# A decoder layer with a mixture of experts: code padding, the final squares, one PSUM bank and three bias loads

## The chip, the cores and the metric

The kernel runs on one core of a Trainium2 chip. TensorE (PE in the profile, PEld for its weight loads) multiplies matrices, VectorE (DVE), ScalarE (ACT) and GpSimd (POOL) do the elementwise work, and SyncE (SP) issues most of the DMAs. Each engine runs its own instruction stream in order, and the streams meet at semaphores. The metric is the device time of one execution in microseconds. Three executions of the kernel before took 2072.66, 2072.96 and 2073.78 us.

## The reference

One layer on 1024 tokens of 1024 features, float32 throughout, and a final RMSNorm:

```
h = rmsnorm(x, norm1_g);  q, k, v, u = split(h @ w_in)            # w_in: 1024 x 2048
attn = differential attention, 4 heads, causal:  softmax(q0 k0) v - lam * softmax(q1 k1) v, then rmsnorm per head
pool = trailing means of u over 2, 4, 8, 16 tokens, minus u, times w_pool, plus b_pool, times pool_scale
x = x + concat(attn, pool) @ w_out
h = rmsnorm(x, norm2_g)
top 4 of 32 experts per token, gates = softmax of the 4 router logits
expert e:  gate = min(h w_gate + b_gate, 7);  up = clip(h w_up + b_up, -7, 7)
           y = (gate * sigmoid(1.702 gate) * (up + 1)) w_down + b_down, times the token's gate
x = x + sum of the expert outputs
return rmsnorm(x, final_g)
```

The final norm needs, for each token, the sum of the squares of its row, the inverse root of the mean (`rstd`), and the product with `rstd` and with `final_g`.

## The kernel before

The tokens are eight blocks of 128 (`TB` = 8). The work has four stages on the time axis of the profile.

**Projection and attention (0 to about 370 us).** `jobs` is a list of TensorE products, each into one PSUM bank: transposes of x, then q, k, v and u. `bank_of(n)` gives the bank of job n: `n % 8` for the early ones, and from `first_late` on (the first block of v is job `first_late`, number 34) alternately two banks, here 1 and 3. Before it writes a bank, PE waits until the last user of that bank has been emptied (`user_before`, `emptied`, in `product`, L1442). Job 33, the last product of k, sits in bank 1 (33 % 8) and is emptied by DVE at L934. Job 27 sits in bank 3.

**Output projection and routing (about 370 to 508 us).** For each block b, PE computes the output projection, DVE adds the residual (`x1_ready`), ACT and DVE make the second norm, PE the router's logits, DVE picks the experts, POOL prepares the gates. SP stores each block's x and h rows to DRAM (L399, L401) and, in its turn for the last block, first waits for `out_mm` and loads the three bias matrices of 32 x 1024 (L397) into rows of `hT`. PE transposes two of them at L1677 once all three have landed (`turn_bias`), then ranks the last block's tokens (L1630). When the routing is done, POOL gathers the first expert's rows (L558).

**Experts (508 to 2054 us).** PE's program holds one body of code for each of 11 widths (128, 132, ... 192 token slots); `choose` (L1749) is a chain of compare-and-branch instructions that jumps to the body of the next expert's width, and each body ends with such a chain. `call` places a prefetch hint (L1760) some time ahead of the branch. A body has six groups of products (L1694, or L1721 at width 128). SP streams the weights. DVE evicts with bias and clip (`gate_in`, `up_in`, `down_in`), ACT does the sigmoid, POOL gathers and scatters rows.

**The end (2031 us on).** When the last but one expert's rows have been added in DRAM, SP reads the eight blocks of x back into `x2` (L439; `x_in[b]` counts the landing of block b). ACT squares and sums each block as it lands (L857, `squares_of_rows`). DVE meanwhile evicts the last expert: `down(0)` and `down(1)` are L1254. After all eight sums, DVE computes `rstd` in 12 small steps (L87 to L100, `rsqrt_mean_dve`). Blocks 0 to 3 (`SCALED` = 4) were multiplied by `final_g` on POOL (L640) and are scaled by ACT (L863); blocks 4 to 7 are done by DVE in one instruction each (`normed_row`, L1363). SP sends the blocks out in a fixed order: 4, 1, 5, 2, 6, 3, 7 (L446 for blocks 4 to 7, L443 for blocks 1 to 3); block 0 goes by an indirect DMA of POOL (L643). The rows of the last expert take a way of their own (`last_rows`): PE transposes the expert's output (L1873) after `down(1)`, DVE adds it to the gathered rows (L1350), ACT squares (L873), DVE makes the inverse root and the product (L1359), and POOL writes those rows over the blocks in `out` (L632), which it may do only after all eight blocks have landed there.

The order on every engine is the order in which the code is written; no scheduler moves it. The two lines that choose the bank and the join before the inverse root are

```
return n % 8 if n < first_late else (1, 3)[(n - first_late) % 2]
dve.wait_ge(squares_f, TB)
```

## Time and profile before

| | before |
|---|---|
| median of 3 runs | 2072.96 us (2072.66 to 2073.78) |
| the profiled execution | 2074.92 us, of which the span of the trace is 2073.2 us |
| PE busy | 2011.8 us, 97% of the span |
| DVE, ACT, POOL busy | 655.5, 283.8, 232.9 us |
| TensorE clock granted | 0.99 of full speed over the span |
| DMA | 500.89 MB, mean 242 GB/s |

PE is busy in all but 61 us of the span, and the experts' stretch is three quarters of it. The profiled execution is 1.96 us longer than the median of the runs; a forecast of a difference is worked out on the profiled execution and then carried to the median.

### The profile page before, as it was taken

To read this page: it belongs to the slowest core of one execution; us is meant where nothing else is said; L and a number is where in the kernel's file an instruction comes from. 1 tells how busy PE (TensorE), PEld (TensorE's weight loads), DVE (VectorE), ACT (ScalarE), POOL (GpSimd) and SP (SyncE) were. 2 spreads that over 40 slices of the span, in tenths; PEclk is the share of its full clock that TensorE was granted. 3 is DMA by queue.
4 is the path that set the end of the run, shared out by engine and by line. 5 is a ranking of instruction groups with operands and counts; after the bars stand their busy time and mean duration, and the time that the engine had idled before them with its cause. 6 is when DMAs were issued, how large, how long until landed. Compare 5 with 4: busy or idle time off the path is not lost.

```text
span 2073.2 us, 32125 instructions
## 1 busy us (share of the span) xinstructions
PE 2011.8 (97%) x13457; PEld 1643.8 (79%) x13458; DVE 655.5 (32%) x1363; ACT 283.8 (14%) x457; POOL 232.9 (11%) x381
## 2 busy tenths in 40 slices
PE   8999988996999999999999999999999999999996
PEld 4444455554998898889788999988888888989996
DVE  3115676443223222222222332222222222222223
ACT  2001245111011001101001010111010100100103
POOL 0001333212000001000001010010000000000103
PEclk9999999997999999999999999999999999999998
DMA  4210022214878879998999988899899998887855
GB/s 173 81 41 1 1 92 84 100 61 152 305 248 305 307 272 322 321 329 296 321 322 318 309 294 272 286 319 335 312 304 322 319 319 310 279 299 260 287 189 199
DMA packets 231449, 500.89 MB, mean 242 GB/s; under 512 B 7766, under 2 KB 8303, under 8 KB 231298
## 3 DMA queue, kind: packets, MB, share of 16 engines
q1 hardware_dynamic: 218880, 454.46, 61.0%
q0 software_dynamic: 12368, 44.26, 8.6%
q8 instruction: 113, 1.85, 0.4%
q14 instruction: 38, 0.31, 0.0%
q10 hardware_dynamic: 50, 0.01, 0.0%
HBM read 463.63 MB, written 35.13 MB: 241 GB/s over the span
## 4 chain that ended last, share of the span: by engine, by line
PE 72%; DMA 1%; DVE 1%; issue 1%; SPq 0%; ACT 0%; POOL 0%; POOLq 0%; DVEq 0%; ACTq 0%
PE ps L1694 57%; PE ps L1721 12%; PE ps L1708 2%; PE ps L1714 1%; PE ps L1701 1%; DMA qk<-x_rows 1%; DMA out<-qk 0%; DVE x L1254 0%; DMA hT<-h_rows,hT 0%; DMA x_rows<-x,hT 0%; DVE qk L1363 0%; SPq L439 0%; DVE xn L1221 0%; ACT hT L821 0%; ACT x L857 0%
## 5 line engine op out<-in xcount | busy, mean ns | idle before, releaser
L1694 PE MATMUL ps<-hT,qk 128*128 128x128 f32 (+8 forms) x4096 | 501.7, 284 | 6.8 <-issue 6.8
L1694 PEld LDWEIGHTS ps<-hT,qk 128*128 128x128 f32 x4096 | 493.5, 192 | 16.6 <-issue 16.0
L1721 PE MATMUL ps<-w_ring,hT 128*128 128x512 f32 x576 | 251.8, 593 | 0.0
L1694 PE MATMUL ps<-hT,u_all 128*128 128x128 f32 (+8 forms) x2048 | 247.7, 282 | 0.0
L1694 PE MATMUL ps<-hT,v 128*128 128x128 f32 (+8 forms) x2048 | 247.7, 282 | 0.0
L1694 PEld LDWEIGHTS ps<-hT,v 128*128 128x128 f32 x2048 | 244.6, 191 | 0.0
L1694 PEld LDWEIGHTS ps<-hT,u_all 128*128 128x128 f32 x2048 | 244.6, 191 | 0.0
L1694 PE MATMUL ps<-hT,w_ring 128*128 128x132 f32 (+7 forms) x1792 | 233.8, 291 | 5.0 <-DVE x L1254 3.6
L1694 PEld LDWEIGHTS ps<-hT,w_ring 128*128 128x128 f32 x1792 | 229.3, 190 | 7.4 <-issue 7.0
L1721 PEld LDWEIGHTS ps<-w_ring,hT 128*128 128x128 f32 x576 | 107.5, 190 | 126.7 <-issue 126.3
L558 POOL DMA_INDIRECT hT<-h_rows,hT x46 | 45.3, 986 | 1148.9 <-issue 672.1
L825 ACT ACTIVATE hT<-hT 128x768 f32<-128x768 f32 x64 | 53.9, 842 | 855.5 <-DVE hT L1235 855.5
L1467 PE MATMUL ps<-hT,w_ring 128*128 128x512 f32 x384 | 168.9, 595 | 1.3 <-DMA w_ring<-in_w_in 1.3
L1467 PEld LDWEIGHTS ps<-hT,w_ring 128*128 128x128 f32 x384 | 71.5, 190 | 86.7 <-issue 83.7
L1241 DVE TENSOR_TENSOR hT<-ps,early 128x512 f32<-128x512 f32 (+1 forms) x64 | 51.7, 808 | 241.3 <-PE ps L1694 234.0
L1232 DVE TENSOR_TENSOR hT<-ps,early 128x512 f32<-128x512 f32 (+1 forms) x64 | 51.7, 808 | 212.9 <-PE ps L1694 191.1
L563 POOL DMA_INDIRECT x_rows<-x,hT x44 | 70.1, 1593 | 266.9 <-ACT x L836 220.1
L821 ACT COPY hT<-ps 128x1024 f32<-128x1024 f32 x64 | 51.2, 800 | 338.8 <-PE ps L1708 298.5
L1262 DVE TENSOR_TENSOR x<-ps,x 128x512 f32<-128x512 f32 x36 | 24.9, 692 | 220.4 <-PE ps L1721 220.4
L1254 DVE TENSOR_TENSOR x<-ps,early 128x768 f32<-128x768 f32 x28 | 26.8, 958 | 193.5 <-PE ps L1694 193.5
L1239 DVE TENSOR_TENSOR hT<-hT 128x512 f32<-128x512 f32 (+1 forms) x64 | 52.4, 818 | 65.8 <-ACT hT L825 65.8
L1203 DVE COPY hT<-ps 128x12 f32<-128x12 f32 x31 | 5.3, 171 | 180.5 <-PE ps L1701 180.5
(250 smaller groups left out, 1470.6 us busy)
## 6 DMA issues: line engine op xcount, KB each, us to landing
w_ring<-in_w_down SPq DMA_DIRECT2D x64, 2048.0 KB, 7.9
qk<-in_w_gate SPq DMA_DIRECT2D x32, 2048.0 KB
qk<-in_w_up SPq DMA_DIRECT2D x32, 2048.0 KB
v<-in_w_gate SPq DMA_DIRECT2D x32, 2048.0 KB, 10.5
u_all<-in_w_up SPq DMA_DIRECT2D x32, 2048.0 KB, 8.7
x<-in_b_down SPq DMA_DIRECT2D x32, 512.0 KB, 11.6
w_ring<-in_w_in SPq DMA_DIRECT2D x3, 2048.0 KB, 9.0
x<-in_x SPq DMA_DIRECT2D x8, 512.0 KB, 12.4
```

The source lines that it names most:

```text
L558: return pool.indirect_dma_start(out=xg[0:n, h, :], out_offset=None, in_=rows.h2[:, :], in_offset=bass.IndirectOffsetOnAxis(ap=tab_e[0:n, ...
L563: return pool.indirect_dma_start(out=rows.x1[:, :], out_offset=bass.IndirectOffsetOnAxis(ap=tab_e[0:n, h:h + 1].bitcast(U32), axis=0), in_ ...
L821: act.copy(xT[:, :, h * P:h * P + n], turned_in[h]).then_inc(xT_ready, 1)
L825: act.activation(sg[:, :, :], gt[:, :, :], ACT.Sigmoid, scale=ALPHA).then_inc(sg_ready, 1)
L1232: dve.tensor_tensor(gt[:, :, 0:n], pair[2 * c % PAIRS][:, :, 0:n], bcast(r.bias[:, 0, 4 * c:4 * c + 4, e], n), ALU.add).then_inc(pair_free, 1)
L1239: dve.tensor_tensor(sg[:, :, 0:n], gt[:, :, 0:n], sg[:, :, 0:n], ALU.mult).then_inc(gate_s, 1)
L1241: dve.tensor_tensor(ut[:, :, 0:n], pair[(2 * c + 1) % PAIRS][:, :, 0:n], bcast(r.bias[:, 1, 4 * c:4 * c + 4, e], n), ALU.add).then_inc(pai ...
L1254: dve.tensor_tensor(yT[:, 4 * c:4 * c + 4, 0:n], pair[(4 + c) % PAIRS][:, :, 0:n], bcast(r.bias[:, 2, 4 * c:4 * c + 4, e], n), ALU.add).th ...
L1467: ins = pe.matmul(bank, ring[:, tile_of[what] % 2, k, a * P:(a + 1) * P], hT[:, k, b * HALF:(b + 1) * HALF], start=k == 0, stop=k == KC - 1)
L1694: ins = pe.matmul(bank[:, m, 0:n], w[g][:, k, m * P:(m + 1) * P], rhs[:, k, 0:n], start=k == 0, stop=k == KC - 1)
L1708: ins = pe.transpose(turned_in[h][:, k, :], xg[0:n, h, k * P:(k + 1) * P], ident[0:n, 0:n])
L1721: ins = pe.matmul(ps[:, 2 * (g % PAIRS), :], aT[:, k, 0:P], w[g][:, k, :], start=k == 0, stop=k == KC - 1)
```

## The change

Four edits go together.

1. **Padding of PE's code.** After the first `choose`, and behind each width's body, a new block is opened and `addr_align(256)` is written in it, which asks that what follows begins at a multiple of 256 instructions.
2. **The squares of the final norm.** ACT squares blocks 0 to 3 only. DVE squares blocks 4 to 7 with `tensor_tensor_reduce` (product and sum in one instruction, the product goes to `junk_v`), ahead of the `rstd` steps. `down(0)` moves from ahead of these to behind the `rstd` steps, and block 7's `normed_row` moves from behind `down(1)` to ahead of it.
3. **The bank of v's first product.** The late jobs alternate between banks 3 and 1 rather than 1 and 3.
4. **The bias loads.** They are issued at b = 5, without a wait of their own, into three other places (`xn[5]`, `hT[4]`, `xn[4]`); the scratch tile `junk_h` moves to `xn[0]`.

```
-        junk_h, ss_h = xn[:, 4], lam[:, 6:7]
+        junk_h, ss_h = xn[:, 0], lam[:, 6:7]
-        bias_rows = flat[0:E, 2 * D:2 * D + 3 * D].rearrange("p (i n) -> p i n", i=3)
+        bias_rows = [xn[0:E, 5], hT[0:E, 4], xn[0:E, 4]]
-            return n % 8 if n < first_late else (1, 3)[(n - first_late) % 2]
+            return n % 8 if n < first_late else (3, 1)[(n - first_late) % 2]
@@ SP
                 for b in range(TB):
-                    if b == TB - 1:
-                        sp.wait_ge(out_mm, 2 * TB)
+                    if b == TB // 2 + 1:
                         for i, bias in enumerate((d["b_gate"], d["b_up"], d["b_down"])):
-                            sp.dma_start(bias_rows[:, i, :], bias[0]).then_inc(biases_in, 16)
+                            sp.dma_start(bias_rows[i], bias[0]).then_inc(biases_in, 16)
@@ ACT
-                    for b in range(TB):
+                    for b in range(TB if again else TB // 2):
...
-                act.wait_ge(squares_f, TB)
+                act.wait_ge(squares_f, TB // 2)
@@ DVE, last expert
-                    normed_row(TB - 1)
                     dve.wait_ge(last_in, 32)
...
-                    down(0)
                     f.n = 0
                     f.did(dve.memset(ss_l, 1.0))
+                    for b in range(TB // 2, TB):
+                        dve.wait_ge(x_in[b], 32)
+                        f.need()
+                        f.did(dve.tensor_tensor_reduce(junk_v, x2[:, b, :], x2[:, b, :], 1.0, 0.0, ALU.mult, ALU.add,
+                                                       accum_out=ss[:, b:b + 1]))
                     dve.wait_ge(gf_in, 16)
-                    dve.wait_ge(squares_f, TB)
+                    dve.wait_ge(squares_f, TB // 2)
                     rsqrt_mean_dve(dve, f, rstd[:, :], ss[:, :], tmp[:, :, :], D)
                     f.need()
                     dve.sem_inc(rstd_f, 1)
-                    for b in range(SCALED, TB - 1):
+                    down(0)
+                    for b in range(SCALED, TB):
                         normed_row(b)
                     down(1)
                     last_rows(nh)
@@ PE
                 choose("first", first, first_hints, len(WIDTHS) - 1)
+                nc.switch_bb("first_pad")
+                pe.addr_align(256)
                 for i, n in enumerate(WIDTHS):
                     with nc.body(place[i], parent=start, valid_engines=[pe.engine]):
                         expert(i, n)
+
+                        nc.switch_bb(f"{place[i]}_pad")
+                        pe.addr_align(256)
```

**PE, from the first `choose` to the first products of the body of width 128.** In the built program before (the line of the code is the first column):

```order
L1725 UNCONDITIONAL_BRANCH
L1729 UNCONDITIONAL_BRANCH
L1749 COMPARE_AND_BRANCH x10
L1753 UNCONDITIONAL_BRANCH
L1772 ISA
L1778 ISA
L1779 ISA
L1694 MATMUL ps<-hT,qk 128x128 x32
```

and in the built program of the change, where the file's lines stand four further on:

```order
L1729 UNCONDITIONAL_BRANCH
L1733 UNCONDITIONAL_BRANCH
L1753 COMPARE_AND_BRANCH x10
L1757 UNCONDITIONAL_BRANCH
L1776 ISA
L1782 ISA
L1783 ISA
L1698 MATMUL ps<-hT,qk 128x128 x32
```

The two `addr_align` lines of the changed file are L1868 and L1874. No row of either line stands here, nor behind any other body: both programs have 1627 rows on PE when waits are told apart, and they differ in the line numbers and in the tile that the bias transposes read.

**DVE, in the last expert at widths above 128, around the added squares** (the difference; `x_in4` to `x_in7` are the landings of blocks 4 to 7, `ISA` with `xn,ss<-qk` is the square with its sum, `ISA ss` reads the sum out):

```order
 L1247 SCALAR_TENSOR_TENSOR hT<-hT 128x768 [waits up_s,gate_s]
-L1254 TENSOR_TENSOR x<-ps,early 128x768 [waits y_ready,group_done]
-L1375 MEMSET x 128x2
+L1373 MEMSET x 128x2
+L1377 ISA xn,ss<-qk 128x1024 [waits order_f,x_in4]
+L1377 ISA ss 128x1
+L1377 ISA xn,ss<-qk 128x1024 [waits order_f,x_in5]
+L1377 ISA ss 128x1
+L1377 ISA xn,ss<-qk 128x1024 [waits order_f,x_in6]
+L1377 ISA ss 128x1
+L1377 ISA xn,ss<-qk 128x1024 [waits order_f,x_in7]
+L1377 ISA ss 128x1
```

Four squares now stand where `down(0)` stood, ahead of the `rstd` steps.

**DVE, behind the `rstd` steps of the same stretch** (the difference; L1254 is `down`, L1362 or L1363 is `normed_row`, L1349 or L1350 the last expert's rows):

```order
 L100 SCALAR_TENSOR_TENSOR rstd<-tmp 128x8 [waits order_f]
-L1363 SCALAR_TENSOR_TENSOR qk<-qk,rstd,g 128x1024 [waits order_f]
-L1363 SCALAR_TENSOR_TENSOR qk<-qk,rstd,g 128x1024 x2
+L1254 TENSOR_TENSOR x<-ps,early 128x768 [waits order_f,y_ready,group_done]
+L1362 SCALAR_TENSOR_TENSOR qk<-qk,rstd,g 128x1024 x4
 L1254 TENSOR_TENSOR x<-ps,early 128x768 [waits y_ready,group_done]
-L1363 SCALAR_TENSOR_TENSOR qk<-qk,rstd,g 128x1024
-L1350 SCALAR_TENSOR_TENSOR x<-ps,hT 128x1024 [waits back_mm0,last_in]
```

Between `rstd` and the first output block there is now one `down`, and between `rstd` and the second `down` there are four `normed_row` instead of three.

**SP, in the stores of the routing stage.** Before, the last blocks:

```order
L401 DMA h_rows<-xn 128x1024 [waits h2_ready]
L397 DMA hT<-in_b_gate 32x1024 [waits out_mm]
L397 DMA hT<-in_b_up 32x1024
L397 DMA hT<-in_b_down 32x1024
L399 DMA x_rows<-x 128x1024 [waits x1_ready]
L401 DMA h_rows<-xn 128x1024 [waits h2_ready]
```

and now, behind block 4 (`hT` in the first row) and ahead of block 5:

```order
L400 DMA h_rows<-hT 128x1024 [waits h2_ready]
L396 DMA xn<-in_b_gate 32x1024
L396 DMA hT<-in_b_up 32x1024
L396 DMA xn<-in_b_down 32x1024
L398 DMA x_rows<-x 128x1024 [waits x1_ready]
L400 DMA h_rows<-hT 128x1024 [waits h2_ready]
```

The three loads have passed two blocks' stores on SP's queue and have lost their wait for `out_mm`.

## Rows read from the trace of the kernel before

**Rows 1.** The page: busy us by engine, and the last chain by engine.

```profile
PE 2011.8 (97%) x13457; PEld 1643.8 (79%) x13458; DVE 655.5 (32%) x1363; ACT 283.8 (14%) x457; POOL 232.9 (11%) x381
...
PE 72%; DMA 1%; DVE 1%; issue 1%; SPq 0%; ACT 0%; POOL 0%; POOLq 0%; DVEq 0%; ACTq 0%
```

**Rows 2.** PE's waits, 520 to 2023 us: total us, times, longest.

```profile
PE ps L1694 <- DVE x L1254: 3.6, 5, 0.8
PE ps L1694 <- issue: 1.4, 4, 0.5
PE ps L1701 <- DVE xn L1221: 0.5, 1, 0.5
```

**Rows 3.** PE's timeline at the first body: start, us, instruction [idle before <-releaser].

```profile
506.85 1.08 PE L1708 MATMUL ps<-ident,hT 64*128 64x64 f32 x8 [1.19 <-ACT hT L821]
514.02 10.40 PE L1694 MATMUL ps<-hT,qk 128*128 128x132 f32 x64 [6.09 <-issue]
...
532.18 7.36 PE L1694 MATMUL ps<-hT,v 128*128 128x132 f32 x64
```

**Rows 4.** The branches of L1749: duration ns min/median/max, first and last start us.

```profile
L1749 PEldq COMPARE_BRANCH  x108: 67/73/6119, 507.3 to 2053.1; - x108
```

**Rows 5.** Timeline around v's first product, 117 to 135 us.

```profile
126.78 0.69 DVE L934 TENSOR_TENSOR qk<-ps,g 128x512 f32<-128x512 f32 x1 [6.17 <-PE ps L1467]
...
127.61 7.11 PE L1461 MATMUL ps<-w_ring,hT 128*128 128x512 f32 x16 [0.88 <-DVE qk L934]
```

**Rows 6.** Timeline around the bias transposes, 491 to 494 us.

```profile
491.42 1.18 PE L1677 MATMUL ps<-ident,hT 32*128 32x32 f32 x16 [0.39 <-DMA hT<-in_b_down]
...
493.50 0.21 PE L1630 MATMUL ps<-member,tri 128*128 128x32 bf16 x1 [0.90 <-DVE member L1118]
```

**Rows 7.** The square on DVE at the program's start, ns: L897.

```profile
L897 DVE CUSTOM_DVE_ANT_0 u_all<-x x4: 1225/1226/1227, 5.9 to 20.0; 128x1024 f32<-128x1024 f32 x4
L897 DVE DVE_READ_ACCUMULATOR2_ANT ss<- x4: 82/84/84, 7.0 to 21.2; 128x1 f32 x4
```

**Rows 8.** Timeline of the end, first part: squares, `down(0)`, POOL's products.

```profile
2039.25 9.31 POOL L640 TENSOR_TENSOR qk<-qk,g 128x1024 f32<-128x1024 f32 x4
...
2046.54 1.06 ACT L857 ACTIVATE x<-qk 128x1024 f32<-128x1024 f32 x1 [2.19 <-DMA qk<-x_rows]
...
2049.02 0.17 DVE L87 TENSOR_SCALAR tmp<-ss 128x8 f32<-128x8 f32 x1 [3.20 <-ACT x L857]
```

**Rows 9.** The same timeline, second part: blocks out and the last rows.

```profile
2051.37 4.27 ACT L863 ACTIVATE qk<-qk,rstd 128x1024 f32<-128x1024 f32 x4 [2.44 <-DVEq L1380]
2051.44 3.68 DVE L1363 SCALAR_TENSOR_TENSOR qk<-qk,rstd,g 128x1024 f32<-128x1024 f32 x3 [0.16 <-DVE rstd L100]
2052.75 0.34 SPq L446 DMA_DIRECT2D out<-qk  x1
...
2055.03 0.95 DVE L1254 TENSOR_TENSOR x<-ps,early 128x768 f32<-128x768 f32 x1
...
2055.90 1.28 DVE L1363 SCALAR_TENSOR_TENSOR qk<-qk,rstd,g 128x1024 f32<-128x1024 f32 x1
2057.09 2.46 DVE L1350 SCALAR_TENSOR_TENSOR x<-ps,hT 128x1024 f32<-128x1024 f32 x2
```

**Rows 10.** The chain that ended last, its final pieces: start, us, what.

```profile
2058.76 7.57 DMA out<-qk
```

**Rows 11.** The same timeline, third part: the last expert's rows.

```profile
2063.06 2.47 DVE L1359 SCALAR_TENSOR_TENSOR hT<-x,g 128x1024 f32<-128x1024 f32 x2
2067.62 0.99 POOL L632 DMA_INDIRECT out<-hT  x1 [12.80 <-issue]
```

**Rows 12.** A window: us, PE, PEld, DVE, ACT, POOL busy, clock, DMA share, GB/s.

```profile
2054.00:2057.00 3.00, 2.36 (x20) 1.98 (x18) 3.00 (x3) 1.64 (x2) 0.81 (x1) 1.00 1.01 386
```

**Rows 13.** A cast on POOL beside a DVE product of two SBUF tiles, and alone.

```profile
484.73 0.63 POOL L534 CAST xn<-gate 128x32 bf16<-128x32 f32 x1
...
485.77 0.29 POOL L534 CAST xn<-gate 128x32 bf16<-128x32 f32 x1
```

8 lines of the change are left out of this document (4 added, 4 removed).

## The prediction

> **What bounds the kernel now.** I read the page first: PE is busy 97% of the span, and the chain that ended last lies on PE for 72% of it [rows 1]. So nothing on the other engines counts unless PE waits for it, or PE has finished. The next view is therefore PE's waits in the experts' stretch: 5.5 us in 1503 us, of which 1.4 us is "issue", the only part that the place of code could be behind [rows 2]. Then the timeline at the four places of the edits. At the jump to the first body PE stands for 6.09 us with nothing that the profile can name, and its next group takes 10.40 us where the same group takes 7.36 us 18 us later [rows 3]. One branch of the 108 at that line took 6.12 us while the median is 0.07 us [rows 4], so the stand is that branch. At the start of v PE waits 0.88 us for DVE [rows 5]. At the bias transposes it waits 0.39 us for the load, and then 0.90 us for DVE [rows 6]. From about 2031 us on the end is a chain of transfers, squares and small steps; PE's own products are over shortly before 2055 us, where DVE's second `down` starts, and the last 18 us belong to the other engines and the DMA queues [rows 9 to 11].
>
> **The padding: 0.** The built program has no row of either `addr_align` line; PE's rows are the same in number and order as before (the first two order listings of the section on the change). Each pad block stands behind an unconditional branch and nothing jumps to it, and in the listing it is gone. No instruction of PE can then stand elsewhere than before, and the 6.09 us stay. Cost and gain 0. If a later step of the build put the padding back, the bounds would be these: a gain of at most the stand, the slow group behind it and the other issue waits, 6.09 + (10.40 − 7.36) + 1.4 = 10.5 us, and a loss of one such 6.1 us branch. I take 0.
>
> The trace shows a jump that costs 6.12 us once and is nearly free in the median [rows 4]. The Trainium skill, on its page "Runtime: NRT & Kernel Launch", section "Instruction fetch mechanics", says that instructions are fetched in blocks of 16 KiB, 256 instructions, and that a taken branch to a block that is not there waits for a DMA. By that rule the trace agrees with a missing block at the first jump, and an aligned body would still be missing from the buffer at that moment, so even a working alignment needn't win the 6 us.
>
> **The bank of v's first product: −0.85.** Before, v's first product waits for bank 1, whose last user, the last product of k, DVE empties from 126.78 to 127.47 us; PE starts v at 127.61 after 0.88 us idle [rows 5]. Now it takes bank 3, whose last user is six jobs older, at some 7 us each, and long emptied. PE can go on at once: 0.03 us between products remain, so 0.85 us is saved. What is late next: the scores behind it need all banks emptied, which was so at 127.5 us and they come 7 us later; the second v product now uses bank 1, also emptied by then. The whole chain behind is tied by semaphores to this one, with ACT, DVE and PE alternating, so the gain should travel to the end. Bounds: −0.88, and 0 if a transfer or a wait further on that keeps its own time swallows it.
>
> **The bias loads: 0.** The wait of 0.39 us goes. But the 0.90 us wait on `member` comes after it and ends at 493.44 us, whatever PE did before [rows 6]; `member` hangs on DVE's logits, which wait for DVE's own norm steps of the last block. PE only waits 1.29 us in one piece instead of two. SP's last x store leaves some 0.6 us earlier, with three issues out of its way, and nobody waits for it: the way on to the first gather leads through `member` and POOL's gates, some 5 us later. The three loads now stand ahead of block 5's stores, where SP is idle waiting for `x1_ready`. Bounds: −0.39 and 0; I take 0.
>
> **The squares on two engines and the moved `down`: +1.0.** This is the step that could go either way, so in order of time.
>
> First the sums. Before, ACT has the last but one square at 2046.54 and the last right behind it, each about 1.2 us with its read-out, and DVE starts the `rstd` steps at 2049.02 [rows 8]. The one at 2046.54 had waited 2.19 us for its block to land, so the landings set this pace, and only the last square, behind the last but one, is ACT's own delay. On DVE a square takes 1.226 + its read-out, together 1.24 us from start to end [rows 7], as long as on ACT. Two of them from 2046.54 with 0.08 us between for the semaphore end at 2046.54 + 2 × 1.24 + 0.08 = 2049.10; the first `rstd` step then starts at 2049.15, 0.13 us later than before. The split moves work, but the blocks that land last are all on one engine still. So it costs 0.13 us and gains nothing.
>
> Then DVE's queue. Before: `rstd` ready, three output blocks from 2051.44, `down(1)`, block 7 from 2055.90, then the last rows from 2057.09 [rows 9]. Now: one `down` of 0.96 us, four blocks at 1.2 us pitch, `down(1)`. So block 4 is ready at 2052.72 + 0.13 + 0.96 = 2053.8 rather than 2052.7, block 5 and 6 are late by the same 1.1 us, block 7 is ready at 2051.44 + 0.13 + 0.96 + 3 × 1.2 + 1.28 = 2057.4, against 2057.18 before. `down(0)` itself delayed nobody before and delays nobody now: PE's transposes need it at 2055, and it is done at 2052.5.
>
> Two paths lead on. The one that ended last goes through the eight blocks: the last `out` transfer is issued at 2058.76 and takes 7.57 us [rows 10], since the DMA engines are full from 2054 on (share 1.01, 386 GB/s [rows 12]). SP's first issue, at 2052.75, waits for block 4 and holds the issues of blocks 1 and 5 behind it. It now leaves at 2053.85, 1.1 us later, but block 1 is then ready at once, and block 0's transfer by POOL leaves as before. So the DMA engines begin to be full 0.6 to 1.1 us later and end so much later: I take +1.0 with the 0.13 in it. The other path is the last expert's rows: `down(1)` ends at about 2058.4 instead of 2055.98, PE's second half of the transposes takes 0.7 us, and the first L1350 starts at 2059.15 instead of 2057.09, +2.1 us. L1359 then ends at 2065.53 + 2.1 = 2067.6 [rows 11]. Before, the eight landings released POOL at 2058.76 + 7.57 = 2066.33 [rows 10] and L632 ran at 2067.62 [rows 11], with both halves needed by about 2067.4, my estimate of where POOL's waits stand ahead of it. With the landings at 2067.3 and POOL's waits over at 2068.4 this path is hidden again. If the landings didn't move it would add 0.2 to 0.5 us by itself. Bounds for the whole step: +0.13 (DMA makes up everything, rows path hidden) and +2.1 (the rows path in full).
>
> A port: a cast on POOL took 0.63 us beside a DVE product of two SBUF tiles, 0.29 us without [rows 13]. DVE's four squares read two SBUF operands beside POOL's four products, which end at 2048.56 [rows 8]. Slowed by all of the squares' time, 4.9 us, they would end at 2053.5; ACT scales four blocks in 4.27 us from 2051.37 [rows 9] and needs the last product for the fourth, at about 2054.5. So it is hidden, by 1 us. The Trainium skill says the same, page "GPSIMD Engine Reference", section "1. Specifications": POOL shares its SBUF interfaces with VectorE and collides with instructions of two SBUF inputs. By that rule the products are late by up to the squares' time, and the sum stays what it was.
>
> **The sum**: 0 − 0.85 + 0 + 1.0 = +0.15 us. On the profiled execution that is 2074.92 + 0.15 = 2075.1; carried to the median of the runs, 2072.96 + 0.15 = 2073.1 us. 0.2% of it, what a measurement of this kernel can tell from no change, is 4.1 us; the three runs of before lie within 1.1 us.
>
> **The rivals.**
> *The padding acts after all.* For it: the diff asks for it, and PE has 6.09 us of stand and 3.04 us of slow products behind it at a jump [rows 3]. Against: the listing has no row of it. The time would be anywhere up to 10.5 us lower; half of it, −5 us, gives 2068.1.
> *The bank's gain alone arrives.* The end is hidden behind the DMA queue: +0.13 and −0.85 give 2072.2. For it: block 7 is ready only 0.2 us later. Against: SP's queue is opened 1.1 us later and the engines are full from then on.
> *Slower: the last rows' path decides.* `down(1)` behind four blocks pushes transposes, L1350, ACT's squares, twelve steps and L1359 by 2.1 us. It decides once its delay exceeds the landings' by 1.9 us, the slack between L1359's end at 2065.53 and the 2067.4 of above. With a DVE slowed by POOL, and the bank's gain lost on the way, it comes to +2.5 us, 2075.5; that is slower than before, yet under the 4.1 us. To be slower by more, a new miss of code on another engine would be needed, DVE's and ACT's programs have changed length at the end, and one branch of 6.12 us [rows 4] shows its price: 2079.
>
> **How the numbers follow.** The forecast 0.58; the gain alone 0.15; the padding acts 0.08; the rows' path 0.14; a new miss 0.05. The first, second and fourth lie within 0.2%, 0.87; of the padding's 0.08 some 0.05 is beyond 4.1 us, to the faster side, and I add 0.01 for what I don't see; the rest is slower. So faster 0.06, same 0.89, slower 0.05. The range takes in 2072.2 and 2075.5 and the spread of runs, about 0.8 us to each side and somewhat more below for a padding that acts in part: 2070.9 to 2076.3.
>
> **What would show it.** Right: no group of PE's with idle before it at v's first product; the 6.1 us stand and the 6.1 us branch unchanged; PE's wait at L1630 about 1.3 us and none at the bias transposes; four squares on DVE of 1.2 us, `rstd` steps starting 2.5 to 2.7 us behind the start of the sixth block's landing, the first `out` issue of SP 3.7 to 4.9 us behind the first `rstd` step, L1350 some 2 us later than before against the end of PE's products, and L632 about 1 us later. Wrong: the stand at the first jump shorter than 4 us (then the padding acts), `rstd` earlier against the last landing than before, or the gain of 0.85 us gone before 500 us.

## The result and the profile after

The change makes the kernel slower: 2078.43 us (2076.86 to 2080.79, 14 runs) against 2073.62 us (2072.06 to 2074.74) for the kernel before in the same rounds, a ratio of 1.0026 with an interval of 1.0018 to 1.0033. That is +4.8 us between the medians and +5.4 us (3.7 to 6.8) by the ratio. The forecast was 2073.1 us, with a range of 2070.9 to 2076.3. The profiled execution after has a span of 2076.9 us against 2073.2.

The page after, against [rows 1], moves nothing that matters: TensorE is as busy, and VectorE is busy for 12 us more, its four squares. Four squares at the price of [rows 7] are 4.9 us; the rest is below.

```profile
PE 2013.0 (97%) x13457; PEld 1645.2 (79%) x13458; DVE 667.6 (32%) x1371; ACT 279.0 (13%) x449; POOL 233.1 (11%) x381
PE 72%; DVE 2%; DMA 1%; issue 1%; ACT 0%; SPq 0%; POOL 0%; ACTq 0%; DVEq 0%; POOLq 0%
```

TensorE's waits from 520 to 2023 us answer [rows 2]; the columns are the waiting operation, what released it, us, times, longest. They are the same to 0.1 us, so the loss is not beside the experts.

```profile
PE ps L1698 <- DVE x L1254: 3.6, 5, 0.8
PE ps L1698 <- issue: 1.3, 4, 0.4
PE ps L1705 <- DVE xn L1221: 0.5, 1, 0.5
```

The timeline of TensorE after, in three stretches (columns as in [rows 3]): v's first product, the place of `member`, and the first body.

```profile
125.58 7.03 PE L1465 MATMUL ps<-w_ring,hT 128*128 128x512 f32 x16
...
491.36 0.21 PE L1634 MATMUL ps<-member,tri 128*128 128x32 bf16 x1 [1.35 <-DVE member L1118]
...
511.85 8.43 PE L1698 MATMUL ps<-hT,qk 128*128 128x132 f32 x46 [6.24 <-issue]
```

v's first product has no idle time ahead of it any more, where [rows 5] had 0.88 us. The two waits of [rows 6], 0.39 and 0.90, have become one of 1.35. The stand at the first body is 6.24 us against 6.09 in [rows 3], and the branch that takes it is still there: its duration now reads 67/73/6279 ns (min, median, max) where [rows 4] has 67/73/6119. The slow group behind the stand, 10.45 us here and 10.40 in before, is TensorE's clock and not its code: TensorE had worked for 3.0 of the 8 us ahead of 508 in before and not at all from there to 514, and the granted clock was 0.50 there and at 514 to 517 us, 0.61 at 517 to 521 and 1.00 from 521 on. Up to here TensorE is 2.2 us ahead of before (511.85 against 514.02). All of that and 3.7 us more are lost in the last 45 us.

The timelines of VectorE and GpSimd from 2034 us on, after (columns as above; the many `rstd` steps left out):

```profile
2038.99 8.40 DVE L1377 CUSTOM_DVE_ANT_0 xn<-qk 128x1024 f32<-128x1024 f32 x1 [4.10 <-DMA qk<-x_rows]
2047.53 1.23 DVE L1377 CUSTOM_DVE_ANT_0 xn<-qk 128x1024 f32<-128x1024 f32 x1
2048.91 1.22 DVE L1377 CUSTOM_DVE_ANT_0 xn<-qk 128x1024 f32<-128x1024 f32 x1
2050.29 1.23 DVE L1377 CUSTOM_DVE_ANT_0 xn<-qk 128x1024 f32<-128x1024 f32 x1
2051.66 0.17 DVE L87 TENSOR_SCALAR tmp<-ss 128x8 f32<-128x8 f32 x1
...
2054.13 0.96 DVE L1254 TENSOR_TENSOR x<-ps,early 128x768 f32<-128x768 f32 x1 [0.21 <-DVE rstd L100]
2055.00 4.86 DVE L1362 SCALAR_TENSOR_TENSOR qk<-qk,rstd,g 128x1024 f32<-128x1024 f32 x4
2059.78 0.95 DVE L1254 TENSOR_TENSOR x<-ps,early 128x768 f32<-128x768 f32 x1
```

```profile
2034.44 1.32 POOL L621 DMA_INDIRECT hT<-x_rows,hT  x1 [8.60 <-issue]
2036.06 0.93 POOL L621 DMA_INDIRECT hT<-x_rows,hT  x1 [0.30 <-issue]
2037.00 9.29 POOL L639 TENSOR_TENSOR qk<-qk,g 128x1024 f32<-128x1024 f32 x4
...
2071.34 0.99 POOL L631 DMA_INDIRECT out<-hT  x1 [14.17 <-DVE hT L1358]
```

This is the place. The first of VectorE's squares starts at 2038.99, within the first of GpSimd's four products, and lasts 8.40 us; the other three last 1.23, the price of [rows 7]. GpSimd's products take 9.29 us for four, as in [rows 8] where no square was beside them: they were not slowed at all. They end at 2046.29, and the square ends 1.1 us behind that, at 2047.39, which is its own 1.1 to 1.2 us of work. The other three squares have had their data for long by then and follow back to back. So the `rstd` steps start at 2051.66.

Since each execution arrives at the end at its own time, I count from GpSimd's first product. In before it starts at 2039.25, the `rstd` steps 9.77 us later at 2049.02 [rows 8], and the span ends 24.2 us after that. After, the two stretches are 14.66 and 25.2 us. The end has lost 4.9 us ahead of the `rstd` steps and 1.1 us behind them. And what ends last is another thing. In before the `out` transfer of [rows 10] stands ahead of GpSimd's last scatters in the chain that ended last. After, the last rows' product on VectorE stands there (start, us, what):

```profile
2069.18 1.27 DVE hT L1358
```

### The profile page after: what moved, and what is told of

Its sections match the earlier page's. It is cut to its first block, busy times and chain, and to the rows that moved or that the text cites. A ratio compares the mean times of both kernels' runs of the same rounds, so it can differ in the third digit from the quotient of the medians.

```text
span 2076.9 us, 32125 instructions
## 1 busy us (share of the span) xinstructions
PE 2013.0 (97%) x13457; PEld 1645.2 (79%) x13458; DVE 667.6 (32%) x1371; ACT 279.0 (13%) x449; POOL 233.1 (11%) x381
## 4 chain that ended last, share of the span: by engine, by line
PE 72%; DVE 2%; DMA 1%; issue 1%; ACT 0%; SPq 0%; POOL 0%; ACTq 0%; DVEq 0%; POOLq 0%
PE ps L1698 57%; PE ps L1725 12%; PE ps L1712 2%; PE ps L1718 1%; PE ps L1705 1%; DVE xn L1377 1%; DMA qk<-x_rows 0%; DVE x L1254 0%; DVE qk L1362 0%; DMA x_rows<-x,hT 0%; DMA hT<-h_rows,hT 0%; DVE xn L1221 0%; SPq L438 0%; ACT hT L820 0%; POOL out L631 0%
## 5 line engine op out<-in xcount | busy, mean ns | idle before, releaser
L1254 DVE TENSOR_TENSOR x<-ps,early 128x768 f32<-128x768 f32 x28 | 26.8, 957 | 186.0 <-PE ps L1698 185.7
## 6 DMA issues: line engine op xcount, KB each, us to landing
v<-in_w_gate SPq DMA_DIRECT2D x32, 2048.0 KB, 10.6
```

The source lines that it names most:

```text
L1254: dve.tensor_tensor(yT[:, 4 * c:4 * c + 4, 0:n], pair[(4 + c) % PAIRS][:, :, 0:n], bcast(r.bias[:, 2, 4 * c:4 * c + 4, e], n), ALU.add).th ...
```

## The experiments

Theory A: a VectorE instruction that reads SBUF is shut out while GpSimd's products follow each other, and that, with the moved `down`, is the whole loss at the end. Rivals: the order of `down` and of block 7 alone (B), the place of the code at the end or in the bodies (C), the moved tiles and loads (D), a loss ahead of the end (E).

**e1, the changed kernel with its end as before.**

```
-                    for b in range(TB if again else TB // 2):
+                    for b in range(TB):
@@ DVE: the squares out, down(0) ahead of the rstd steps, normed_row(7) behind down(1)
```

> The changed kernel with its end put back as it was before (all eight squares on ACT, the downs and block 7 in their old places); padding lines, bank and bias loads stay as changed. Theory A, the square of block 4 on VectorE is held up beside GpSimd's products and costs the end all it lost: the time is that of the kernel before minus about 1 us (the wait at v's first product), 0.9995 of it, and PE's last products come some 1 us earlier than in before. Theory B, the loss is from the padding, the bias loads or code that stands elsewhere: this kernel is slower than before by 3 to 5 us. Theory C, the end's transfers were only unlucky in the profiled execution: as A, but then the end alone won't cost anything either.

Measured: 2071.85 us, 0.9993 of before (0.9984 to 1.0002). GpSimd's first product to the `rstd` steps 9.79 us, from there to the end 24.1. All of the loss is in the end; padding, bank and loads cost nothing that the times can show.

**e2, the kernel before with the end edit alone** (the same lines the other way round).

> The kernel before with the end's edit alone (four squares on VectorE, moved downs, block 7 ahead of the second down). Theory A: slower than before by 5 to 6 us, ratio about 1.0028; the first square on VectorE takes about 8 us again, as long as GpSimd's products run. Theory B: within 1 us of before. Theory C: within 1.5 us of before, and the first square takes 1.2 us.

Measured: 2079.25 us, 1.0029 (1.0019 to 1.0040); the stretches are 14.65 and 25.2 us. Its timeline of VectorE has the same stand:

```profile
2039.54 8.35 DVE L1378 CUSTOM_DVE_ANT_0 xn<-qk 128x1024 f32<-128x1024 f32 x1 [4.15 <-DMA qk<-x_rows]
2048.04 1.23 DVE L1378 CUSTOM_DVE_ANT_0 xn<-qk 128x1024 f32<-128x1024 f32 x1
```

**e3, the kernel before with the moved `down(0)` and block 7, all squares on ScalarE.**

```
-                    down(0)
                     f.did(dve.memset(ss_l, 1.0))
...
                     dve.sem_inc(rstd_f, 1)
-                    for b in range(SCALED, TB - 1):
+                    down(0)
+                    for b in range(SCALED, TB):
```

> The kernel before with the new order on VectorE alone: all eight squares stay on ACT, the first down stands behind the rstd steps, block 7 ahead of the second down. It tells how much of the end's loss is the order. Theory A (port): the rstd steps start as before and the end is later by 0.6 to 2.1 us, as I had worked out for this part, less than half of the loss. Theory D (the order is the loss: the last expert's rows wait for the second down behind four blocks): slower by 4 us or more.

Measured: 2074.1 us, 1.0003 (0.9994 to 1.0012). From the `rstd` steps (2047.63) to the end (2072.9) 25.3 us against 24.2 before: the order costs 1.1 us in the trace, which the times can't tell from nothing. Rival B falls as the cause of the loss. One thing to keep for later: from GpSimd's first product to the `rstd` steps it is 10.6 us here (from 2037.02), 9.8 in before and e1 and 9.4 in e5, none of which has a square on VectorE, so that stretch is known to about 1 us.

**e4, the changed kernel without GpSimd's four products** (blocks 0 to 3 lack the factor `final_g`).

```
-                        pool.tensor_tensor(x2[:, b, :], x2[:, b, :], g2[:, :], ALU.mult).then_inc(times_g, 1)
```

> The changed kernel without GpSimd's four products with final_g (blocks 0 to 3 of the output lack that factor); nothing else of it changes. Theory A: the four squares on VectorE take 1.23 us each and start as their blocks land, the rstd steps start some 2.6 us behind the sixth landing, and the kernel is some 2.5 us faster than the changed kernel as profiled, to within 1.5 us of before. Theory E (the square is slow for another reason, a late transfer or the place it writes to): the first square stays at 8 us and the time stays 4 to 6 us above before.

Measured: 2072.93 us, 0.9999 (0.9990 to 1.0008). Its timeline of VectorE:

```profile
2039.38 1.22 DVE L1373 CUSTOM_DVE_ANT_0 xn<-qk 128x1024 f32<-128x1024 f32 x1 [4.39 <-DMA qk<-x_rows]
2041.79 1.23 DVE L1373 CUSTOM_DVE_ANT_0 xn<-qk 128x1024 f32<-128x1024 f32 x1 [1.18 <-DMA qk<-x_rows]
2044.52 1.22 DVE L1373 CUSTOM_DVE_ANT_0 xn<-qk 128x1024 f32<-128x1024 f32 x1 [1.49 <-DMA qk<-x_rows]
2045.89 1.23 DVE L1373 CUSTOM_DVE_ANT_0 xn<-qk 128x1024 f32<-128x1024 f32 x1
2047.26 0.17 DVE L87 TENSOR_SCALAR tmp<-ss 128x8 f32<-128x8 f32 x1
```

With the products away each square lasts 1.23 us and waits only for its block to land. The `rstd` steps start 2.74 us behind the start of the last but one square, which waited for its landing; the prediction had said 2.5 to 2.7. In before it is 2.48 us on ScalarE [rows 8]. So the sum for the squares was nearly right for an engine that is let in: 0.26 us in place of 0.13. Counted from GpSimd's second gather, the last thing ahead of its products, the `rstd` steps come 11.1 us later here and 15.6 us later in the change: the products' presence costs 4.5 us.

**e5, the bank alone, on the kernel before.**

```
-            return n % 8 if n < first_late else (1, 3)[(n - first_late) % 2]
+            return n % 8 if n < first_late else (3, 1)[(n - first_late) % 2]
```

> The kernel before with one edit of the change: v's first product writes bank 3, so the order of its banks is 3, 1, 3, 1 and not 1, 3, 1, 3. In the two traces compared so far the stand of 2.1 us behind that product's start shrank and TensorE was 1.04 us further. Theory (the bank is the whole of the gain ahead of the end): 1.0 us less, 2072.6 where the kernel before has 2073.6, and TensorE stays 1.0 us ahead up to the experts. Rival (the gain came from the bias loads or from the start of the program, which varies): no change, 2073.6, and TensorE at the same place as before from 130 us on. Rival (something else ends the span in that stretch, and the gain is given back at v's last product): TensorE ahead at 128 us and level at 300.

Measured: 2072.55 us, 0.9996 (0.9987 to 1.0005): −0.8 us, inconclusive by the times. The traces tell it, if one counts from VectorE's eviction of the last product of k (L934), which starts when that product is done. V's first product starts 0.83 us behind it in before (127.61 against 126.78) and 0.84 in e3, e7b and e12, which have the old banks; it starts 0.20 us ahead of it here (126.17 against 126.37), in the change and in e1. So the bank wins 1.03 us. From v's first product to the first body it is then 386.4 us in before, 386.3 in the change, 386.1 here and 386.0 in e3: the gain is not lost on the way, to within the spread of that stretch, some 0.5 us.

**e6, the kernel before with padding that is carried out,** ahead of each `choose`'s last branch.

```
+                    pe.addr_align(256, offset=255, max_nops=0)
                     branch = pe.br(place[last])
```

> The kernel before with filler instructions put ahead of the last branch of each choice of width, where they are executed (the padding of the change lies behind a branch, in blocks that nothing enters, and is not in the built program). Each width's body then does begin at a multiple of 256 instructions. Theory (where a body begins is of no weight, its code is there before the branch or the wait is a fixed one): 2073.6 within 2, since up to 255 fillers of a few ns on TensorE's queue at 108 choices lie beside 19 us of products for each expert; the stand at the first body stays 6.1 us. Rival (beginning at such a multiple saves a fetch for each body): the stand at the first body falls from 6.1 us toward nothing and the time by 3 to 6 us, 2068 to 2070. Rival (the fillers are paid for at the first choice, or at each): 2 to 10 us more.

Measured: 2077.87 us, 1.0021 (1.0012 to 1.0030), 4.4 us more. The first body's stand is 5.98 us and the fetches of TensorE's instructions fall from 113 to 108 packets, but no time is won. The fillers are not what costs: they stand ahead of each chain's last alternative, which TensorE reaches once, at 2058.4 us, when the experts are done. The comparing branches of L1749 show the price:

```profile
L1749 PEldq COMPARE_BRANCH  x108: 67/73/6870, 507.8 to 2058.3; - x108
```

In before one of them took over 3 us, the first [rows 4]. Here six did: 6.01 us at 508, and 5.39, 6.21, 6.23, 6.31 and 6.87 us at 708, 896, 1122, 1460 and 1730. In before the same five branches took 0.44, 1.64, 0.23, 1.34 and 0.73 us. Most of such a branch is hidden behind the products that TensorE has still queued, 7.13 us of them in front of the last of the five. What is left shows behind it as a wait that before does not have:

```profile
1737.44 2.82 PE L1694 MATMUL ps<-hT,qk 128*128 128x160 f32 x19 [1.31 <-DVE x L1262]
```

The view names VectorE, but the branch ended at 1736.98, so it is the branch. By the starts of the branches around them these five cost some 2.8 of the 4.7 us that this kernel loses between the first body and the last branch; the rest is spread over small steps and was not traced to a cause. So moving the bodies made five more slow branches and took away none.

**e7b, the kernel before with the first hints given later.**

```
-                call(first_hints, first, 0, len(WIDTHS) - 1)
@@ behind the gate's products
+                call(first_hints, first, 0, len(WIDTHS) - 1)
                 pe.wait_ge(gate_read, 1)
```

> The kernel before with the hints for the first expert's code moved: they are given at 498 us and are now given behind the gate's products, some us ahead of the branch. In the trace of before no fetch of TensorE's instructions follows the hint at 498 us, the next one is at 511 us, behind the branch; beside the experts a fetch follows each hint by 1.4 us. Theory (the early hint has no effect because other code is fetched after it, a late one works): the stand of 6.1 us at the first body falls below 2, the products behind it keep the full clock level, which were some 3 us longer at half of it, and the time falls by 4 to 9 us, to 2065 to 2070. Rival (the stand is not the fetch of the first body, or the hint is useless wherever it stands): 2073.6 within 1, and the stand stays 6.1 us. Rival (the stand is hidden behind the gather of the first expert's tokens): the stand falls and the first product starts no earlier.

Measured: 2072.79 us, 0.9997 (0.9988 to 1.0006); the stand is 5.61 us. It told nothing of late hints, though: the wait that the hints had moved past is short, and they were issued at 497.93 us, where before has them at 498.01. Nor does a fetch follow each hint by 1.4 us beside the experts, as the expectation says: in before the next fetch comes 0.5 to 4.1 us behind 19 of the 33 hints and 49 us and more behind seven. e12 moves the hint in earnest.

**probe, what each kind of instruction does beside GpSimd's products.**

> A kernel of its own that leaves out the whole computation: on tiles of 128 x 1024 in SBUF VectorE does three instructions and GpSimd four products of two SBUF tiles beside them, in sections that start together. VectorE's are, by section: a square with sum (two SBUF operands) alone; the same beside GpSimd; a product of two tiles; a product with a constant and a tile; a product of one tile with a constant; a product of a PSUM and an SBUF tile; the square beside GpSimd's product of one tile with a constant; the square beside GpSimd's products that each wait for the one ahead; then two copies on ScalarE beside GpSimd; GpSimd alone; and the square with GpSimd starting behind its first. Theory (a VectorE instruction that reads two SBUF operands is held as long as GpSimd's products follow each other, GpSimd isn't slowed): squares, product and product with constant and tile 1.2 us alone, and the first of each beside GpSimd 8 to 10 us; the forms with one SBUF operand 0.6 to 1.2 us in both; GpSimd's product 2.35 us everywhere. Rival (the two share by turns): each VectorE instruction 2 to 2.5 us and GpSimd's up to 3.6. Rival (only the square with its sum is held): the plain product keeps its 1.2 us. With gaps between GpSimd's products the theory has the square enter at the first gap, so 2.5 to 3.6 us and not 8.

Measured: GpSimd alone takes 2.34 us for a product. Rows of its timeline of VectorE (three instructions each, the first of which starts ahead of GpSimd):

```profile
26.05 7.78 DVE L93 TENSOR_TENSOR vo<-c,e 128x1024 f32<-128x1024 f32 x3 [4.58 <-issue]
38.42 7.78 DVE L95 SCALAR_TENSOR_TENSOR vo<-c,e 128x1024 f32<-128x1024 f32 x3 [4.59 <-issue]
50.79 6.18 DVE L97 TENSOR_SCALAR vo<-c 128x1024 f32<-128x1024 f32 x3 [4.59 <-issue]
61.56 3.49 DVE L99 TENSOR_TENSOR vo<-ps,e 128x1024 f32<-128x1024 f32 x3 [4.58 <-issue]
```

The product of two SBUF tiles and the one with a constant cost 1.23 + 3.36 + 3.36; a tile times a constant, one operand, 0.69 and 2.8 twice; with one operand in PSUM nothing is lost. So a f32 instruction with one SBUF operand is held too. Beside GpSimd's product of one tile with a constant the squares took 1.23, 2.05 and 1.21 us, hardly held. But the theory's 8 us did not come: the two take turns, a whole instruction each, and GpSimd's products take 3.3 us. This contradicted the kernel, where the square passes three boundaries between products without its turn.

**e8, the changed kernel with GpSimd's products waiting for each other.**

```
+                        if b:
+                            pool.wait_ge(times_g, b)
                         pool.tensor_tensor(x2[:, b, :], x2[:, b, :], g2[:, :], ALU.mult).then_inc(times_g, 1)
```

> The changed kernel with a wait ahead of each of GpSimd's products with final_g but the first: for its own last product to be written. Before it they ran back to back, and VectorE's first square stood 8.40 us beside them and ended 1.1 us behind the fourth. Theory (a VectorE instruction that comes while they run gets in only where GpSimd makes a pause): the square starts at 2039.0 within a product and ends 1.1 us behind the end of that product, so it lasts 1.3 to 3.5 us; those that come while products still run last up to 3.4 each; GpSimd's products take up to 3.3 us and end at 2049 or 2050; the rstd steps start at 2047 to 2049 and not at 2051.7, and the time falls from 2078.4 by 2 to 4 us, to 2074 to 2076. Rival (the hold has nothing to do with pauses): the first square lasts 8 us and more, until the fourth product has ended, and the time is 2078.4 or more.

Measured: 2077.27 us, 1.0018 (1.0009 to 1.0027). The squares last 1.40, 2.29, 2.48 and 3.14 us, GpSimd's later products 3.15. The stand is gone, yet the `rstd` steps come 13.47 us behind the first product, and the time is above the 2074 to 2076 expected: taking turns is hardly cheaper than being shut out, 1.2 us.

**e9, the changed kernel with two products on GpSimd.**

```
-SCALED = 4
+SCALED = 2
```

> The changed kernel with SCALED 2 in place of 4: GpSimd does the product with final_g for two blocks, and VectorE does two more blocks whole (1.23 us each, on its path of the end). Theory (the hold ends with GpSimd's last product): that product ends 4.65 us earlier, at 2041.7, the first square lasts 3.75 us in place of 8.40, the other three follow their data, the last ending at 2047.2, so the rstd steps start at 2047.3 and not 2051.7. Behind them come two more rows of 1.2 us on VectorE: 1.9 us less in all where the outs follow VectorE, 2076.5 or less. Rival (the hold has a length of its own or comes from the square's place in SBUF): it lasts 8.40 us, the rstd steps start at 2051.7, and the time rises by 2.4 us to 2080.8.

Measured: 2074.86 us, 1.0009 (1.0000 to 1.0018). The timeline of VectorE and GpSimd:

```profile
2037.73 4.38 DVE L1377 CUSTOM_DVE_ANT_0 xn<-qk 128x1024 f32<-128x1024 f32 x1 [3.52 <-DMA qk<-x_rows]
```

```profile
2036.34 4.68 POOL L639 TENSOR_TENSOR qk<-qk,g 128x1024 f32<-128x1024 f32 x2
```

The square again ends 1.1 us behind GpSimd's last product (2041.02), so the stand has no length of its own. It is as long as the products that follow. The `rstd` steps come 10.0 us behind the first product; from there to the end it is 26.6 us, since VectorE scales two more blocks.

**best, e1 with the hints of e7b.**

> The changed kernel with its end as in the kernel before (all squares on ScalarE, the last block's row behind the second down) and with the hints for the first expert's code moved behind the gate's products. Its two parts alone stood at 0.9993 (end undone) and 0.9997 (hints) of the kernel before. Theory (the bank gives 1.0 us, the hints 0.6 us through the time in which TensorE issues them ahead of a gate's product, and both add): 2071.2 to 2072.0, ratio 0.9990 to 0.9994. Rival (the two stand in one wait for the gather of the first expert's tokens and one hides the other): 2072.3, ratio 0.9995 or more.

Measured: 2072.36 us, 0.9996 (0.9987 to 1.0005). It beats the change, and can't be told from before; nor can e1. Its branch took 5.61 us.

**probe2, VectorE coming in the midst of the products.**

> A kernel of its own that leaves out the whole computation: on tiles of 128 x 1024 f32 GpSimd does six products of two SBUF tiles, and VectorE comes in their midst: it waits for the first of them, does a copy into PSUM (1.2 us), then two squares with sum, in sections. Sections: as said; without the copy, so that VectorE comes right behind a boundary; GpSimd's products in place; GpSimd's products each behind a wait that is already met; both; both, with VectorE waiting for its own last instruction as the kernel does; the last with products, and with one operand and a constant, in place of the squares; the last with three products in place of six; and with GpSimd waiting for its own last product. In the first such kernel, where VectorE's first instruction started before GpSimd's, the two took turns: each product 3.3 us, each square 3.35 us, and no square stood for longer. Theory (coming while GpSimd holds the port is what lets it keep the port over the boundaries): in all sections with six products the first square lasts until 1.1 us behind the sixth, 8 to 11 us, with three products 2 to 4 us, with waits of GpSimd for its own last product 3.4 us. Rival (products in place, or waits that are met, make the difference): only the sections with that show it. Rival (the two always take turns, and the 8.40 us of the kernel come from something this kernel lacks, such as transfers or ScalarE): every square up to 3.4 us.

Measured: no square over 3.35 us in any section, GpSimd's products 3.32 where they meet one. Theory and first rival fall; the two take turns in every section.

**e10, the changed kernel with the first square behind GpSimd's first product.**

```
+                        if b == TB // 2:
+                            dve.wait_ge(times_g, 1)
```

> The changed kernel with one more wait ahead of VectorE's first square: for the first of GpSimd's four products with final_g. So the square starts 0.1 to 0.3 us into the second product, at 2039.4, and not 0.4 us ahead of the end of the first. Theory (the stand comes from starting within the first product, which the kernels of their own with later starts did not do): the square lasts 3.2 us, as there, and the rstd steps start at 2047 to 2049. Rival (where it starts is of no weight): it lasts until 1.1 us behind the fourth product, 8.0 us, and the rstd steps start at 2051.7 as before. Rival (starting right behind a boundary it meets another's turn): 5.6 us, one product longer.

Measured, in one execution: the square starts 0.18 us into the second product and lasts 7.87 us, again until 1.1 us behind the fourth. Whether it starts in the first or the second is of no weight.

**probe3, with ScalarE, transfers and TensorE beside.**

> A kernel of its own that leaves out the whole computation: on tiles of 128 x 1024 f32 GpSimd does four products in place, the first behind ScalarE's first square, and VectorE two squares with sum behind ScalarE's second or third square, so that the first comes within GpSimd's first product. Sections: 1.0 us into it; 2.3 us into it, as in the kernel; the same without GpSimd waiting for ScalarE's later squares; with eight of ScalarE's squares in place of four; with four transfers of 512 KB from HBM beside; with 24 products of TensorE beside; with all of these. Theory (a start within the first product is what makes the stand): 8 us or more in all sections. Rival (the semaphores from ScalarE that GpSimd's products wait for): 8 us in all but the third. Rival (transfers, TensorE or the longer run of ScalarE): 8 us only where that is beside. Rival (none of these): no square over 3.4 us anywhere, and what it is stays open.

Measured: the first squares last 2.29 to 3.30 us in all seven sections. Neither semaphores, transfers from HBM nor the other engines make the stand.

**probe4, tiles at the kernel's places, and gathers ahead of the products.**

> A kernel of its own that leaves out the whole computation: four products of GpSimd in place and two squares with sum of VectorE that come within the first or second, with the tiles allocated in the order and sizes of the kernel's, so that rows of x2, final_g, the square's operand and what it writes have the kernel's names and places. Sections: as in the kernel; with two gathers that GpSimd issues ahead of the products, as there; products on other tiles; square on other tiles; the square written to another tile. Theory (places in SBUF, of which the other kernels had others): 8 us in the first section, and 3.3 us in at least one of the last three. Rival (the gathers): 8 us in the second alone. Rival (neither): no square over 3.4 us, and what it is stays open.

Measured. The first two sections in its timelines of GpSimd and VectorE:

```profile
27.53 11.22 POOL L80 TENSOR_TENSOR qk<-qk,g 128x1024 f32<-128x1024 f32 x4 [26.57 <-ACT x L91]
29.86 3.41 DVE L103 CUSTOM_DVE_ANT_0 xn<-qk 128x1024 f32<-128x1024 f32 x1 [5.03 <-ACT x L91]
33.42 3.13 DVE L103 CUSTOM_DVE_ANT_0 xn<-qk 128x1024 f32<-128x1024 f32 x1
...
39.62 1.12 POOL L74 DMA_INDIRECT hT<-in_x,idx  x1 [0.88 <-issue]
...
41.05 0.94 POOL L74 DMA_INDIRECT hT<-in_x,idx  x1 [0.30 <-issue]
...
42.01 9.23 POOL L80 TENSOR_TENSOR qk<-qk,g 128x1024 f32<-128x1024 f32 x4
...
42.60 9.73 DVE L103 CUSTOM_DVE_ANT_0 xn<-qk 128x1024 f32<-128x1024 f32 x1 [6.05 <-ACT x L91]
...
52.48 1.22 DVE L103 CUSTOM_DVE_ANT_0 xn<-qk 128x1024 f32<-128x1024 f32 x1
```

Here is the stand, in one execution and one section. Without gathers ahead the four products take 11.22 us and the squares 3.41 and 3.13. With two gathers issued by GpSimd right ahead, the products run through in 9.23 us and the square stands 9.73, until 1.1 us behind the last. The three sections that followed, each with one set of tiles elsewhere and without gathers, were as the first (3.13 to 3.27 us). In the kernel two gathers, of the last expert's rows, stand right ahead of the products.

**e11, the changed kernel with one pause, ahead of the second product.**

```
+                        if b == 1:
+                            pool.wait_ge(times_g, b)
```

> The changed kernel with one wait of GpSimd for its own last product, ahead of the second of the four; the third and fourth follow back to back. Theory (GpSimd keeps the way to SBUF from its gathers on, over every boundary, until it once pauses; behind a pause the two take turns, as in the kernels of their own): the first square enters at the pause, 1.4 to 2.5 us, none of the others lasts over 3.4, GpSimd's later products take up to 3.3 us, the rstd steps start at 2048 to 2050 and not at 2051.7, as in e8 (the waits ahead of all: 1.0018 of before). Time 2075 to 2077.5. Rival (back-to-back products keep it at every boundary in this kernel, gathers or not): the first square enters at the pause, but the second stands until 1.1 us behind the fourth product, 4 us or more, and the third product takes its 2.35 us.

Measured: 2077.05 us, 1.0016 (1.0007 to 1.0025). The timeline of VectorE:

```profile
2036.97 1.64 DVE L1379 CUSTOM_DVE_ANT_0 xn<-qk 128x1024 f32<-128x1024 f32 x1 [3.95 <-DMA qk<-x_rows]
2038.88 3.02 DVE L1379 CUSTOM_DVE_ANT_0 xn<-qk 128x1024 f32<-128x1024 f32 x1 [0.26 <-DMA qk<-x_rows]
2042.32 2.88 DVE L1379 CUSTOM_DVE_ANT_0 xn<-qk 128x1024 f32<-128x1024 f32 x1 [0.41 <-DMA qk<-x_rows]
2045.35 3.14 DVE L1379 CUSTOM_DVE_ANT_0 xn<-qk 128x1024 f32<-128x1024 f32 x1
2048.64 0.17 DVE L87 TENSOR_SCALAR tmp<-ss 128x8 f32<-128x8 f32 x1
```

GpSimd's third and fourth products follow back to back and take 3.33 us each: behind one pause the two take turns in this kernel as in the small ones. The `rstd` steps come 13.5 us behind the first product, as in e8. The rival, a hold at every boundary without a pause, falls.

**e12, the kernel before with the hints behind the first transposes.**

```
-                call(first_hints, first, 0, len(WIDTHS) - 1)
...
                 turn_in(0).then_inc(turn_mm[0], 1)
+                call(first_hints, first, 0, len(WIDTHS) - 1)
                 pe.wait_ge(gathered, 32)
```

> The kernel before with the hints for the first expert's code moved behind the transposes of its first tokens: issued at about 505.7 us, where before has them at 498.0 and the branch is at 507.4. In before the gate's product waits 2.5 us for the hints' instructions, and the second transposes wait 1.19 us for ScalarE, beside which the hints would now stand. Theory (a hint that comes late fetches the body, which is what the branch stands for): the fetch of TensorE's instructions comes at 507 us and not at 511.0, the branch takes 3 to 4.5 us in place of 6.12, time −1.5 to −3, 2070.5 to 2072. Rival (hints to this body do nothing): the branch takes 5.6 to 6.3 us and the next fetch follows it; the branch itself comes 0.5 us earlier or later, time within 1 us of before.

Measured: 2068.81 us, 0.9980 (0.9971 to 0.9989): 4.1 us less by the ratio and 4.5 between the medians, more than the 1.5 to 3 us expected. The hint is issued at 503.97, fetches of 16 KiB of TensorE's instructions follow at 504.50 and 505.47, and the branch at 506.35 takes 2.20 us in place of 6.12. The timeline of TensorE:

```profile
502.78 1.94 PE L1708 MATMUL ps<-ident,hT 128*128 128x128 f32 x8 [5.13 <-DMA hT<-h_rows,hT]
505.91 1.08 PE L1708 MATMUL ps<-ident,hT 64*128 64x64 f32 x8 [1.19 <-ACT hT L821]
509.12 8.96 PE L1694 MATMUL ps<-hT,qk 128*128 128x132 f32 x64 [2.12 <-issue]
517.91 0.69 PE L1701 MATMUL ps<-hT,xn 128*128 128x6 bf16 x16
```

The stand is 2.12 us against 6.09 [rows 3]. The slow group behind it takes 8.96 us against 10.40, but in e7b, with the old stand, it takes 8.88, so that is not the hint's doing. So the stand at the first body is for its greater part the fetch of its code, which the hint at 498 us had not brought: the next fetch behind that hint is at 510.99, 3.6 us behind the start of the branch. What the remaining 2 us are was not looked into.

**best2, e1 with the hints of e12.**

> The changed kernel with its end as before and with the hints behind the first transposes, as in e12. Theory (bank 0.8 to 1.0 us, late hint 1.5 to 3 us, and both add): 2069.5 to 2071.5, ratio 0.9982 to 0.9989. Rival (the hint does nothing): as e1, 0.9993.

Measured: 2067.90 us, 0.9973 (0.9963 to 0.9983), with a stand of 2.89 us; 2069.5 to 2071.5 had been expected. It beats before by 5.6 us by the ratio (5.4 between the medians) and lies 10.5 us below the changed kernel's median, which was measured in other rounds.

## Why the prediction was wrong

**The padding, 0: right.** The stand (6.24 us), the branch and TensorE's waits are as before. The bound of a gain, 10.5 us, was too wide: 3.04 us of it are the clock (granted 0.50 behind the stand), which no place of the code gives back. e6 moves the bodies and loses 4.4 us; e12 wins 4.1 to 4.5 us at that branch by the place of a hint. The Trainium skill, page "Runtime: NRT & Kernel Launch", section "Instruction fetch mechanics", says that a taken branch to a block that is not there waits for a DMA. e12 agrees: with two fetches started ahead of it, the branch takes 2.20 us in place of 6.12.

**The bank, −0.85: right in kind, mis-sized by a little.** The idle time of 0.88 us is gone, and v starts 1.03 us earlier against the product ahead of it (e5). In the times −0.8 us can't be shown.

**The bias loads, 0: right**, to the letter: one wait of 1.35 us for `member` in place of two.

**The order of `down` and block 7, +0.87 of the +1.0: the number was right, the path only in part.** Between the `rstd` steps and the end e3, e2, e4 and the change all have 25.2 or 25.3 us where before, e1 and e5 have 24.1 or 24.2: +1.1. In e4 the `out` transfers end last, as forecast: the last landing is 18.4 us behind the first `rstd` step against 17.3 in before. In the change, e2 and e3 it is the last rows' path, which the prediction called hidden. L1358 starts 16.3 us behind the first `rstd` step against 14.0, +2.3 where +2.1 was forecast. But the slack was 1.2 us and not the 1.9 of the prediction: in the change the scatter starts 0.9 us behind the end of L1358, in before 2.1 us behind the end of L1359. 2.3 less 1.2 is again 1.1. That both paths come to the same number is luck.

**The squares, +0.13 and at most hidden: this is the step that failed.** The prediction reads: "Two of them from 2046.54 with 0.08 us between for the semaphore end at 2046.54 + 2 × 1.24 + 0.08 = 2049.10", with 1.24 from a stretch in which GpSimd was not beside [rows 7]. And in the paragraph on the port: "Slowed by all of the squares' time, 4.9 us, they would end at 2053.5 ... So it is hidden, by 1 us." I had seen the collision in [rows 13], and let GpSimd pay for it, since [rows 13] shows a GpSimd instruction that is slowed. In the change GpSimd pays nothing (9.29 us for four) and VectorE pays 7.17 us on one square, 8.40 − 1.23; VectorE is the one of the two on the path. Counted against before, the `rstd` steps are 14.66 − 9.77 = 4.9 us late, not 0.13; against e4 they are 4.5 us late. e4 is the proof that it is the products: with them away, the loss is away.

The Trainium skill, page "GPSIMD Engine Reference", section "1. Specifications", says that GpSimd shares its SBUF interfaces with VectorE and contends with VectorE instructions in a 2-port perf mode or with two SBUF inputs. The runs agree: instructions of two SBUF operands were held, one with an operand in PSUM was not (probe). The f32 instruction of one SBUF operand that lost 2.1 us took 0.69 us alone, where the others took 1.23; whether it runs in a 2-port mode, the trace does not say. That section does not say who pays. By the runs either can, and behind gathers it is VectorE alone.

**The sum.** −1.0 for the bank, +1.1 for the order, +4.9 for the squares (4.5 to 4.9): +5.0 us, against 4.8 between the medians and 5.4 by the ratio (3.7 to 6.8). The rivals that were named missed it too. The one of the last rows' path does name a VectorE slowed by GpSimd, but without a term for it, and stops at 2075.5; the one that was slower by more than 0.2% had the size, 2079, but needed a new miss of code, and e4, with the same code but for the products, is back at the time of before. The prediction bounded the cost to GpSimd's products (0 and 4.9 us) and gave VectorE's squares no upper bound. Held until the products' end at 2048.56 [rows 8], and then 1.1 us and three squares at 1.38 us, they would have ended near 2053.8, 4.8 us later than before: an estimate of 2077.8 us, in whose spread the measured time lies.

What is not settled: why gathers ahead make GpSimd keep its way to SBUF. The runs show that they do in a small kernel (probe4) and that one pause ends it in this one (e8, e11). No run took the gathers out of this kernel, so that they are the cause here too rests on the likeness of the two. Whether another instruction does the same, and how long after a gather it lasts, was not tried.

## What to carry to other kernels

Before work is moved to an idle VectorE, look at what GpSimd does in the same stretch: if both read their operands from SBUF, bound the moved instruction from above by the length of GpSimd's whole run, and not by its own (1.23 us became 8.40 here, and 3.1 to 3.4 where the two took turns). A collision has two sides; put a bound on each engine's instructions, and take the one on the path first. And where the profile shows a stand behind a branch with nothing to name it, look whether a fetch of code follows the hint or the branch, and try the hint at another place.
